# Forget attention: the normalisation of the probabilities moves from the output gate into the products that turn them

## The reference, cut to what matters

```python
def fox_attention(q, k, v, dcum):
    # for each block of 128 queries:
    logits = einsum('bhqd,bhkd->bhqk', qi, k) * scale
    logits = logits + di[..., :, None] - dcum[..., None, :]
    logits = where(kpos <= qpos, logits, -inf)
    p = softmax(logits, axis=-1)
    return einsum('bhqk,bhkd->bhqd', p, v)

def fox_mixer(h, w_qg, q_norm_g, w_o, k, v, dcum):
    ...
    gate = sigmoid(qg[..., D_MODEL:])
    o = fox_attention(q, k, v, dcum) ...
    return (o * gate) @ w_o
```

## Time and profile before

| | |
|---|---|
| time of three executions | 1937.31, 1937.37, 1938.23 us, median 1937.37 |
| profiled execution | 1936.47 us, of which the span from the first to the last instruction is 1934.8 |
| TensorE's granted clock, mean | 0.998 of full speed |
| busy share of the span | TensorE 98%, GpSimd 50%, VectorE 41%, ScalarE 38% |
| the stage (first score 913.50 to the first full projection product 990.81) | 77.3 us; busy in it: TensorE 74.4, ScalarE 57.1, VectorE 54.0, GpSimd 36.8 |
| DMA in the stage | 117 GB/s |

### The profile page before, as it was taken

The page is one execution under the profiler, slowest core; times in us unless marked ns, Lnnn a source line. Parts: engine busy times, 40 slices in busy tenths (PEclk is TensorE's granted clock), DMA queues, the critical chain, the costliest instruction groups (busy, mean ns, idle before and its releaser), DMA issues. The chain is left out here.

```text
span 1934.8 us, 27078 instructions
## 1 busy us (share of the span) xinstructions
PE 1894.6 (98%) x10430; PEld 1592.0 (82%) x10430; DVE 783.9 (41%) x1390; ACT 730.8 (38%) x1197; POOL 959.4 (50%) x550
## 2 busy tenths in 40 slices
PE   7999999999999999999999999999999999999998
PEld 4998887888887878988578888888786988776998
DVE  5676543543344245544735010110227770127213
ACT  4324324422222255455746222222344323447335
POOL 1535654555555445575534555554443443557652
PEclk9999999999999999999999999999999999999999
DMA  9554542566656323235512333323232334321232
GB/s 352 166 168 156 173 166 92 178 186 195 184 182 213 127 77 89 77 95 147 152 56 88 98 98 97 94 92 98 81 87 76 92 101 96 90 78 39 66 104 94
DMA packets 223718, 236.98 MB, mean 122 GB/s; under 512 B 16288, under 2 KB 184008, under 8 KB 223352
## 3 DMA queue, kind: packets, MB, share of 16 engines
q1 hardware_dynamic: 218784, 219.57, 37.5%
q10 hardware_dynamic: 4824, 15.88, 2.5%
HBM read 232.63 MB, written 2.79 MB: 122 GB/s over the span
## 5 line engine op out<-in xcount | busy, mean ns | idle before, releaser
L843 POOL TENSOR_TENSOR w_lo<-raw,w_hi 128x1024 fp32r<-128x1024 f32 (+1 forms) x296 | 719.4, 2444 | 500.4 <-ACT w_hi L836 485.5
L1569 PE MATMUL acc<-hh,w_hi 128*128 128x512 f32 (+1 forms) x1472 | 552.6, 375 | 6.4 <-POOL w_lo L843 3.7
L1569 PE MATMUL acc<-hh,w_lo 128*128 128x512 f32 (+1 forms) x1472 | 546.0, 371 | 0.0
L1569 PE MATMUL acc<-hl,w_hi 128*128 128x512 f32 (+1 forms) x1472 | 545.8, 371 | 0.0
L836 ACT ACTIVATE w_hi<-raw 128x1024 fp32r<-128x1024 f32 (+1 forms) x292 | 304.1, 1052 | 406.6 <-DMA raw<-in_ffn_w_down 158.6
L1569 PEld LDWEIGHTS acc<-hh,w_hi 128*128 128x128 f32 x1472 | 277.3, 188 | 62.7 <-issue 14.1
L1569 PEld LDWEIGHTS acc<-hh,w_lo 128*128 128x128 f32 x1472 | 277.3, 188 | 48.3
L1569 PEld LDWEIGHTS acc<-hl,w_hi 128*128 128x128 f32 x1472 | 277.5, 189 | 46.0 <-issue 0.2
L2158 DVE SCALAR_TENSOR_TENSOR ada_wide<-ada_raw,c_act,ada_wide 128x1024 f32<-128x1024 f32 x84 | 154.1, 1834 | 147.4 <-DMA ada_raw<-in_ada_w 116.9
L1569 PE MATMUL acc<-w_hi,hh 128*128 128x256 f32 x672 | 191.8, 285 | 0.0
L1569 PE MATMUL acc<-w_hi,hl 128*128 128x256 f32 x672 | 190.1, 283 | 0.0
(11 more groups left out here) (551 smaller groups left out, 2839.4 us busy)
## 6 DMA issues: line engine op xcount, KB each, us to landing
raw<-in_ffn_w_gu SPq DMA_DIRECT2D x176, 256.0 KB, 3.2
raw<-in_w_in SPq DMA_DIRECT2D x52, 512.0 KB, 3.6
ada_raw<-in_ada_w SPq DMA_DIRECT2D x50, 512.0 KB, 6.4
raw<-in_ffn_w_down SPq DMA_DIRECT2D x44, 512.0 KB, 3.6
raw<-in_a_w_in SPq DMA_DIRECT2D x32, 512.0 KB, 3.7
ada_raw<-in_ada_w ACTq DMA_DIRECT2D x30, 512.0 KB, 5.6
raw<-in_a_w_out SPq DMA_DIRECT2D x16, 512.0 KB, 3.7
ada_raw<-in_kv_ada_w SPq DMA_DIRECT2D x16, 512.0 KB, 5.4
```

The source lines that it names most:

```text
L843: eng.tensor_tensor(w_lo[:, s, part, :], raw[:, s, part, :], w_hi[:, s, part, :].bitcast(F32), ALU.subtract).then_inc(w_split, 1)
L1569: ins = pe.matmul(out, w, x, start=first and n == 0, stop=last and n == len(pairs) - 1, skip_group_check=check)
```

## The change

In the forget attention the probabilities are no longer turned by a transpose against the identity, but by a product with a diagonal matrix that holds the inverse row sums of the block: that turns and divides at once. VectorE makes these diagonals, one instruction of 128x512 a head, before the groups of that head may start. The spreading of the sums (ScalarE), the four transposes of it (TensorE) and its product with the gate (VectorE) fall away; the output is the product with the values times the gate. The other attention keeps the old way.

```diff
+        FOX_DIAG = [[inv_diag[:], gate_row[:].rearrange("p (b t) -> p b t", b=NB)],
+                    [sq[:, 0, :].rearrange("p (b t) -> p b t", b=NB), sq[:, 1, :].rearrange("p (b t) -> p b t", b=NB)]]
# ScalarE
-                widen(i)
+                if a is dx:
+                    widen(i)
# TensorE, transposes(i, n)
-                pe.wait_ge(a["e_ready"], head_logits(a, i, 0 if n < 2 else 1))
-                if n == 4:
-                    pe.wait_ge(a["e_ready"], head_logits(a, i, 0))
+                if a is fx:
+                    pe.wait_ge(a["dg_ready"], 2 * i + (1 if n < 2 else 2))
+                else:
+                    ...
-                        last = pe.transpose(out[:, c:c + P], buffer_of(a["p"], i)[e][:, ...], ident[:])
+                        src = buffer_of(a["p"], i)[e][:, OFF[b] + s * P:OFF[b] + (s + 1) * P]
+                        if a is fx:
+                            last = pe.matmul(out[:, c:c + P], src, FOX_DIAG[i % 2][e][:, b, :], start=True, stop=True)
+                        else:
+                            last = pe.transpose(out[:, c:c + P], src, ident[:])
...
-                spread_sums(i)
+                if a is dx:
+                    spread_sums(i)
# VectorE
             def copy(i, e):
                 dve.wait_ge(a["t_ps"], 5 * i + 2 * e + 1)
                 dve.tensor_copy(a["pT"][:, e, 0:T], aux[:, 0, :]).then_inc(a["pt_dve"], 1)
+                if a is dx:
+                    dve.reciprocal(rowinv[:, e, :], rowsum[:, e, :]).then_inc(a["sum_read"], 1)
+            def diagonals(i, e):
+                dve.wait_ge(a["e_ready"], head_logits(a, i, e))
                 dve.reciprocal(rowinv[:, e, :], rowsum[:, e, :]).then_inc(a["sum_read"], 1)
+                dve.drain()
+                dve.tensor_tensor(FOX_DIAG[i % 2][e], ident[:].unsqueeze(1).broadcast_to([P, NB, P]),
+                                  rowinv[:, e, :].unsqueeze(2).broadcast_to([P, NB, P]), ALU.mult).then_inc(a["dg_ready"], 1)
...
-                dve.tensor_tensor(tmp[:, c % 4, :], O_BANK[:], a["scaled"][:], ALU.mult).then_inc(t_ready, 1)
+                dve.tensor_tensor(tmp[:, c % 4, :], O_BANK[:], a["scaled"][:] if a is dx else a["gate"][:, i, :], ALU.mult).then_inc(t_ready, 1)
...
             soft(0, a["first_order"])
+            if a is fx:
+                diagonals(0, 0)
             for i in range(a["pairs"]):
                 ...
                 copy(i, 0)
+                if a is fx:
+                    diagonals(i, 1)
                 if more:
                     soft(i + 1, a["order"][0])
                 copy(i, 1)
                 if more:
                     soft(i + 1, a["order"][1])
                 copy_both(i)
-                scaled_gate(i)
+                if a is dx:
+                    scaled_gate(i)
                 if more:
                     soft(i + 1, a["order"][2])
+                if a is fx and more:
+                    diagonals(i + 1, 0)
```

More of the change, by code:

```diff
@@ L346, in build_program @@
             a["rb_in"] = [sem(f"{kind}_rb_in{n}") for n in range(2)]
-            for n in ("mb_ready", "s_ps", "lg_ready", "e_ready", "t_ps", "pt_act", "pt_dve", "r_ps", "scaled_ready", "o_ps", "sum_read"):
+            for n in ("mb_ready", "s_ps", "lg_ready", "e_ready", "t_ps", "pt_act", "pt_dve", "o_ps", "sum_read") + (("dg_ready",) if a is fx else ("r_ps", "scaled_ready")):
                 a[n] = sem(f"{kind}_{n}")
@@ L674, in transposes @@
                 out, c = aux[:, n % 2, :], 0
-                pe.wait_ge(a["e_ready"], head_logits(a, i, 0 if n < 2 else 1))
-                if n == 4:
-                    pe.wait_ge(a["e_ready"], head_logits(a, i, 0))
+                if a is fx:
+                    pe.wait_ge(a["dg_ready"], 2 * i + (1 if n < 2 else 2))
+                else:
+                    pe.wait_ge(a["e_ready"], head_logits(a, i, 0 if n < 2 else 1))
+                    if n == 4:
+                        pe.wait_ge(a["e_ready"], head_logits(a, i, 0))
                 if n % 2 == 0:
@@ L680, in transposes @@
                         pe.wait_ge(a["pt_dve"], 3 * i + n // 2)
+                elif a is fx:
+                    if i or n == 3:
+                        pe.wait_ge(a["pt_act"], 2 * i + n // 2)
                 elif n == 1:
@@ L687, in transposes @@
                     for b in range(s, NB):
-                        last = pe.transpose(out[:, c:c + P], buffer_of(a["p"], i)[e][:, OFF[b] + s * P:OFF[b] + (s + 1) * P], ident[:])
+                        src = buffer_of(a["p"], i)[e][:, OFF[b] + s * P:OFF[b] + (s + 1) * P]
[3 more added lines that the diff above has]
+                            last = pe.transpose(out[:, c:c + P], src, ident[:])
                         c += P
@@ L700, in values @@
                 pe.wait_ge(a["pt_dve"], 3 * i + 2)
+                if a is fx:
+                    pe.wait_ge(a["pt_act"], 2 * i + 2)
                 if i:
@@ L770, in output @@
                 free_tmp_of(dve, c)
-                dve.wait_ge(a["scaled_ready"], i + 1)
                 dve.wait_ge(a["o_ps"], i + 1)
-                dve.tensor_tensor(tmp[:, c % 4, :], O_BANK[:], a["scaled"][:], ALU.mult).then_inc(t_ready, 1)
+                if a is dx:
+                    dve.wait_ge(a["scaled_ready"], i + 1)
+                dve.tensor_tensor(tmp[:, c % 4, :], O_BANK[:], a["scaled"][:] if a is dx else a["gate"][:, i, :], ALU.mult).then_inc(t_ready, 1)
             soft(0, a["first_order"])
+            if a is fx:
+                diagonals(0, 0)
             for i in range(a["pairs"]):
```

## The result

The change makes the kernel slower. Four executions of it took 1951.11, 1951.16, 1954.06 and 1955.50 us, median 1952.61; before, four took 1936.27 to 1938.23, median 1937.34. The ratio is 1.0081 with a 95% interval of 1.0068 to 1.0094, that is +13 to +18 us. The forecast was 1938.8 and its range ended at 1941.0.

The account below looks back on a forecast made before the run. TensorE was taken to pace odd pairs, the mask loop pairs 2, 4 and 6. Pair 6 at +1.5, pair 7 at +2.2, last pair -0.53, weight loads +0.1: about +1.7, taken as +1.4, 1938.8 us; range 1935.9 to 1941.0.

Parts of the forecast that it names:

- Transposes become products with a diagonal ... Taken: nothing: TensorE's 20 transposes a pair: products claimed to run at the same pace, 0.117 us each, so no added time.
- TensorE-paced period: Odd pairs, paced by TensorE's own work: two diagonals less the gate product claimed +0.58 us, 8.6 in place of 8.03.
- The mask loop: Pairs 2, 4 and 6 wait for mask rows fetched into reused buffers, 18.06 us for two pairs; claimed to keep pacing.
- The port: VectorE's diagonals and GpSimd's masks take turns at SBUF: first logits about 0.6 us later, mask blocks 3.9 to 4.5.
- signs of being wrong: Odd periods under 8 us, products pacing at 0.19, or mask-row landings moving by more than 2 us.
- The new products run at the pace of their weight load: TensorE: 192 ns in place of 117 a product, +5.5 us, 1942.9; chance 0.08, shared with a longer VectorE chain.
- the very most (4.2): Rival that TensorE paces every pair: dropping the sums' four transposes saves 0.53 us each pair, -4.2, 1933.1; chance 0.05.

## Why the prediction was wrong, point by point

**The step that failed** is "Transposes become products with a diagonal ... Taken: nothing". The pace was read rightly: 0.117 us for an instruction of either kind; measured in long rows, 0.112 for an instruction of a product and 0.109 for a transpose. What was not read was how many instructions a product is. The row "x16" of the earlier trace rows was called "16 such products"; it is eight. The program at that line makes 8 chunks of 4 blocks, 32 products, and the trace has 64 instructions there. The line of the product with the values says the same: 8 products a pair in the program, x16 in the earlier trace rows. So the term is 20 x 0.117 = +2.3 us a pair for TensorE in place of nothing. Put into the prediction's own sum it gives: TensorE's work per pair 7.94+2.3-0.53 = 9.8 us (9.92 measured without diagonals), no mask waits, 7 x 9.8 - 61.0 = +7.6 and +1.8 in the last pair, +9.4; measured +10.1.

**The diagonals cost more behind double products than alone.** The prediction gave them +0.58 us in a TensorE-paced period. With transposes the periods are 8.5 to 9.1 us and one of 9.6, but only +1.3 in all for the whole stage, as the diagonals use up waits for masks. In after they cost 0.6 to 0.8 in every period, since no mask wait is left to hide them, 5.3 us. The mechanism is the one that was named (the diagonal is the last thing on VectorE, and TensorE stands idle for it), its cover is gone.

**The mask loop** was read rightly: the third set of buffers took it away and gave 3.5 and 5.4 us in two measurements, 5.5 in the trace. That the change would still be paced by it was wrong, because of the failed step: in after the masks of pairs 4 and 6 start at 949.70 and 971.60, 3 and 7 us later than before, which is one of the signs of being wrong that the prediction named.

**The port** was read rightly: 3.79 to 3.83 us for most blocks of eight masks, the lower end of the forecast 3.9 to 4.5 not quite reached, since only one diagonal pushed most blocks back. In after it is a small part of the loss, some 1.2 us of it in the last five full periods. What the walk left out is that a diagonal can also meet a longer GpSimd instruction: beside a split of weights it took 2.30 us, and no term of the prediction stands for that.

**The rivals.** "The new products run at the pace of their weight load" had the sign and the place, with the wrong cause and a third of the size. The Trainium skill, TensorE: Matmul & The Clock Gate, "Terms", has the transpose mode as 4 times faster for FP32. The runs show a factor of 2 in the count of instructions and none in the pace of one. I set the sentence aside because a row seemed to deny it, and the row did not; weighed at even a part of its claim it would have pointed to the side on which the time came out.

What stays open: two of after's four executions are 3 and 4 us longer than the other two, at a mean clock of 0.997 and 0.995 (0.998 and 0.997 for the others), and only a short one has a trace. The kernel before shows the same relation: of 27 executions in one session, the five with a mean clock of 0.995 took 1938.99 to 1941.08 us, the five with 0.998 or 0.999 took 1935.29 to 1935.84. What makes the clock fall in some executions no run shows.

## What to carry to other kernels

Before a trace is used as a price list, divide: instructions at a line in the trace by operations at that line in the program. A count per operation of 2 is invisible in every duration and every pace, and here it was 2.3 us a pair. And folding a scale into a transpose can only be free where product and transpose are the same number of instructions; in f32 it doubles them, in the rounded type it does not (and there the diagonals still left +2.4 us). A stage that looks bound by its busiest engine can be paced in every second turn by a double-buffered transfer; a third buffer gave 3.5 to 5.4 us here, about what the change could have saved at the very most (4.2). Where two engines take turns at the memory, the price of a meeting is the length of the other engine's instruction: list them all, and not only those of the loop.

## What the runs showed of the hardware

- An f32 product of 128x128 is two matrix instructions and an f32 transpose one, each at 0.11 us in a row: 200 in 22.50 us, 100 in 11.08. In the rounded type (fp32r) a product is one: 160 for 160.
- The weight load of 192 ns against 140 for the transpose does not show in the pace (0.112 against 0.109 us).
- A VectorE instruction with two SBUF operands beside GpSimd's masks costs each side one turn: 3.34 us for eight masks became 3.80 with one diagonal in between, and 4.25 in the block of after at 971.60, where two fall into it (971.68 and 974.72). The instruction that waits gets its turn at the end of the current one and does not wait for the whole series. Its price is therefore the rest of the current GpSimd instruction: diagonals took 0.72 to 1.01 us beside masks of 0.42 us, and 2.30 and 2.80 beside a weight split of 2.35 (0.69 alone).
- In the two executions traced with rounded products TensorE's clock fell to its half level within this stage (with three mask sets 0.84 of full over 935 to 965 us, with two 0.50 over 970 to 973). Ahead of the first fall TensorE had waited 2.45 us in the one, and only 0.62 and 0.35 in the other. In after, before and the variants with f32 transposes or products it stayed at full level there; the variant with transposes has as many instructions and as long waits as the one with rounded products and two mask sets, so the waits alone do not make it fall, and the cause stays open.
